# Position bias in eight transfers a layer, and VectorE's roots and rotary embeddings behind the attention weights

## The reference, cut to what matters

```python
def hybrid_layer(x, ...):                     # two of them
    h = rms_norm(x, norm_mix_g) * (1 + sc_m) + sh_m      # scale and shift come from c @ ada_w
    # one wide product h @ w_in gives q, k, v of three attentions, latents, and three gates
    o_na  = neighborhood_attention(...)       # 4 heads of 64, on a grid of 8 rows x 64 columns
    o_mla = blocked_attention(...)            # 4 heads, keys and values from a latent of 128
    o_gqa = blocked_attention(...)            # 8 query heads, 2 key heads, axial rotary embedding
    merged = sigmoid(ga)*(o_na @ w_br_na) + sigmoid(gb)*(o_mla @ w_br_mla) + sigmoid(gc)*(o_gqa @ w_br_gqa)
    x = x + g_m * (merged @ w_out)
    ...                                       # then a gated feed-forward block

def neighborhood_attention(q, k, v, rpb):     # rpb: (4 heads, 15 row offsets, 31 column offsets)
    s = einsum(q_row, k_band) * scale         # 16 queries of a row against 8 rows x 32 columns
    s = s + rpb[:, row_off][..., col_off]     # position bias
    s = where(col_valid, s, -inf)             # a window of 16 columns
    p = softmax(s)
```

## Time and profile before

| what | value |
|---|---|
| median of three runs | 2883.03 us |
| the profiled execution: its own time | 2883.88 us |
| the profiled execution: its span | 2882.1 us |
| granted TensorE clock, mean | 0.994 |
| VectorE busy | 1545.7 us (54%) |
| ScalarE busy | 677.5 us (24%) |
| GpSimd busy | 1659.0 us (58%) |
| DMA | 280.49 MB, mean 97 GB/s |
| `rpb_wide<-bias_copies` | 64 transfers of 24.0 KB |

### The profile page before, as it was taken

How to read it: one execution, slowest core, us unless ns; L and a number is a source line. 1 busy time by engine, 2 the same in 40 slices (tenths; PEclk the granted TensorE clock), 3 DMA queues, 4 the chain that set the end, 5 groups by cost and what they waited for, 6 DMA issues and landing times.

```text
span 2882.1 us, 44383 instructions
## 1 busy us (share of the span) xinstructions
PE 2825.3 (98%) x18030; PEld 2243.4 (78%) x18030; DVE 1545.7 (54%) x2283; ACT 677.5 (24%) x1158; POOL 1659.0 (58%) x1332
## 2 busy tenths in 40 slices
PE   8899999999999999999999999999999999999998
PEld 6666787888877767778888877877777787788886
DVE  6788876555225664444333275655566456662342
ACT  3444212000014443111000033233333433310000
POOL 4434577877765334586777744344344534676774
PEclk9999999999999999999999999999999999999999
DMA  7323543344332112232223221122112212222221
GB/s 278 106 94 125 195 163 125 138 153 148 129 103 80 37 59 67 72 118 85 98 95 102 98 82 49 59 67 69 56 62 69 70 47 69 81 95 95 99 98 59
DMA packets 97524, 280.49 MB, mean 97 GB/s; under 512 B 21278, under 2 KB 32286, under 8 KB 97182
## 3 DMA queue, kind: packets, MB, share of 16 engines
q1 hardware_dynamic: 85904, 274.70, 28.0%
q10 hardware_dynamic: 11438, 3.26, 0.6%
HBM read 275.76 MB, written 3.13 MB: 97 GB/s over the span
## 4 chain that ended last, share of the span: by engine, by line
PE 89%; DVE 7%; issue 1%; ACT 1%; ACTq 1%; DMA 0%; SPq 0%; DVEq 0%; POOL 0%; POOLq 0%
PE ps L358 25%; PE ps L360 24%; PE ps L359 24%; PE ps L1404 3%; PE ps L1212 2%; PE ps L1222 2%; PE ps L1242 2%; ACTq L618 1%; PE ps L1449 1%; DVE first_mod L1718 1%; PE ps L1037 1%; PE ps L1033 1%; PE ps L1034 1%; PE ps L1526 0%; DVE mg L1812 0%
## 5 line engine op out<-in xcount | busy, mean ns | idle before, releaser
L592 POOL TENSOR_TENSOR wR<-raw,wR 128x512 fp32r<-128x512 f32 (+1 forms) x866 | 1198.9, 1403 | 68.0 <-ACT wR L649 31.0
L588 POOL CAST wR<-raw 128x1024 fp32r<-128x1024 f32 (+3 forms) x462 | 465.8, 1008 | 1123.6 <-PE ps L360 1005.5
L358 PE MATMUL ps<-hR,wR 128*128 128x512 f32 x2224 | 903.8, 406 | 7.0 <-DVE hR L1739 6.8
L359 PE MATMUL ps<-hR,wR 128*128 128x512 f32 x2224 | 870.1, 391 | 0.0
L360 PE MATMUL ps<-hR,wR 128*128 128x512 f32 x2224 | 869.4, 391 | 0.0
L358 PEld LDWEIGHTS ps<-hR,wR 128*128 128x128 f32 x2224 | 419.2, 188 | 113.3 <-issue 21.6
L360 PEld LDWEIGHTS ps<-hR,wR 128*128 128x128 f32 x2224 | 419.1, 188 | 89.9
L359 PEld LDWEIGHTS ps<-hR,wR 128*128 128x128 f32 x2224 | 419.8, 189 | 82.2 <-issue 4.3
L1697 DVE SCALAR_TENSOR_TENSOR xT<-ps,lm,xT 128x512 f32<-128x512 f32 x32 | 24.0, 751 | 215.4 <-PE ps L360 215.4
L358 PE MATMUL ps<-act_f,wR 128*128 128x512 f32 x352 | 137.7, 391 | 0.0
L360 PE MATMUL ps<-act_f,wR 128*128 128x512 f32 x352 | 137.0, 389 | 0.0
(11 more groups left out here) (394 smaller groups left out, 4180.7 us busy)
## 6 DMA issues: line engine op xcount, KB each, us to landing
raw<-in_weights_dram SPq DMA_DIRECT2D x468, 512.0 KB, 3.3
first_mod<-in_weights_dram SPq DMA_DIRECT2D x16, 512.0 KB, 10.4
raw<-in_weights_dram SPq DMA_DIRECT2D x50, 128.0 KB, 2.4
raw<-in_weights_dram SPq DMA_DIRECT2D x16, 256.0 KB, 2.9
raw<-in_weights_dram SPq DMA_DIRECT2D x8, 384.0 KB, 10.4
xT<-in_x_dram SPq DMA_DIRECT2D x1, 2048.0 KB, 9.6
out_dram<-xT SPq DMA_DIRECT2D x4, 512.0 KB, 2.6
rpb_wide<-bias_copies ACTq DMA_DIRECT2D x64, 24.0 KB, 2.7
```

The lines of the kernel that those rows point to most:

```text
L358: mm(out, w_hi, r_hi, start=first, stop=False)
L359: mm(out, w_hi, r_lo, start=False, stop=False)
L588: nc.gpsimd.tensor_copy(wR[:, u, 0, 0:cols], raw[:, r % RING, 0:cols]).then_inc(hi_done, 1)
L592: ins = nc.gpsimd.tensor_tensor(wR[:, u, 1, part], raw[:, r % RING, part], wR[:, u, 0, part], ALU.subtract)
```

## The change

It does four things in each of the two hybrid layers.

1. The padded bias rows in DRAM are 64 elements wide (16 zeros, 31 values, 17 zeros), not 127. `rpb_wide` takes whole rows of 64, so that one piece of 8 rows x 64 elements (2 KB) is contiguous, and one transfer brings all four heads of a query row: 8 transfers of 128 KB a layer take the place of 32 of 24 KB. They are issued at the same places, 4 and 4.
2. Before step 0 VectorE masks only kinds 0 and 1 of pair 0. Kind 2 of pair 0 and all of pair 1 come in `between(1)`, ahead of `outputs(0)`.
3. `gk_root` (step 2), `rope(10)` (step 4) and `q_root(3, ...)` (step 6) move from `between` to `behind`, that is behind `weights_of`.
4. A late post whose next product is a short one (fewer than eight steps) goes ahead of `modulate`.

```diff
-BIAS_ROWS = 4 * 15 * 127
+BIAS_ROWS = 4 * 15 * 64
-NA_WIDE = 48
+NA_WIDE = 64
-    dram_bias = nc.dram_tensor("bias_rows", (DEPTH * 4 * 15, 127), F32, kind="Internal")
+    dram_bias = nc.dram_tensor("bias_rows", (DEPTH * 4 * 15, NA_WIDE), F32, kind="Internal")
-                rows = sb("rows", [DEPTH * 60, 127], into=r)
+                rows = sb("rows", [DEPTH * 60, NA_WIDE], into=r)
-            act.dma_start(rows[:, 48:79], rpb).then_inc(s_rows, 16)
+            act.dma_start(rows[:, NA_COLS:NA_COLS + 31], rpb).then_inc(s_rows, 16)
...
                 for row in range(first_row, end):
-                    for h in range(4):
-                        first = NA_COLS * BIAS_ROWS * l + (h * 15 + 7 - row) * 127 + GRID - 1 - NA_COLS
-                        act.dma_start(rpb_wide[16 * row:16 * row + 16, h],
-                                      bass.AP(dram_copies, first, [[BIAS_ROWS - 1, NA_COLS], [127, 8], [1, NA_WIDE]])).then_inc(s_bias, 16)
+                    first = NA_COLS * BIAS_ROWS * l + (7 - row) * NA_WIDE + NA_COLS - 1
+                    act.dma_start(rpb_wide[16 * row:16 * row + 16].rearrange("p h k e -> p h (k e)"),
+                                  bass.AP(dram_copies, first, [[BIAS_ROWS - 1, NA_COLS], [15 * NA_WIDE, 4], [1, 8 * NA_WIDE]])
+                                  ).then_inc(s_bias, 16)
...
-                def mask_bias(pair):
+                def mask_bias(pair, kinds):
-                    dve.wait_ge(s_bias, 512 * l + 512)
+                    dve.wait_ge(s_bias, 128 * l + 128)
-                    for kind, first in enumerate(BAND_TABLE):
+                    for kind in kinds:
+                        first = BAND_TABLE[kind]
...
-                mask_bias(0)
+                mask_bias(0, (0, 1))
...
                 def between(s):
-                    if s == 2:
-                        gk_root()
+                    if s == 1:
+                        mask_bias(0, (2,))
+                        mask_bias(1, (0, 1, 2))
                     elif s == 3:
                         ckv_root()
-                    elif s == 4:
-                        rope(10)
-                    elif s == 6:
-                        q_root(3, 0, 12, ((0, 8, 0.125), (8, 12, 96 ** -0.5)))
...
                 def behind(s):
                     if s == 2:
+                        gk_root()
                         rope(14)
                     elif s == 3:
                         latent(8, 7)
                     elif s == 4:
+                        rope(10)
                         latent(6, 2)
                     elif s == 5:
                         latent(7, 3)
                     elif s == 6:
+                        q_root(3, 0, 12, ((0, 8, 0.125), (8, 12, 96 ** -0.5)))
                         kr_rope()
...
-                    if s == 1:
-                        mask_bias(1)
                     behind(s)
+                    late = [p for p, early in ENDS[s] if not early and PRODS[p][0] in GATE_OF]
+                    soon = [p for p in late if PRODS[p + 1][2] < KD]
+                    for p in soon:
+                        post(p)
                     if l == 0:
                         rows_done = modulate(rows_done, DUE["step", s])
-                    for p, early in ENDS[s]:
-                        if not early and PRODS[p][0] in GATE_OF:
+                    for p in late:
+                        if p not in soon:
                             post(p)
```

## The result

| kernel | median us (lowest to highest, runs) | ratio to before, 95% interval |
|---|---|---|
| before | 2882.90 (2880.27 to 2886.25, 4) | |
| after | 2865.78 (2864.57 to 2867.14, 4) | 0.9942 (0.9930 to 0.9955) |

The change saves 17.1 us (0.58%), more than the 0.2% that can be told from nothing. The profiled execution of after took 2864.96 us, 18.9 less than that of before; its span is 2863.2 us.

The account below looks back on a forecast made before the run. TensorE, busy 98%, was taken as the bound, so time is won only from its stalls and low clock; 7.1 + 0.8 + 5.9 + 0.8 + 0.2 + 2.2 = 17.0 us off 2883.9 gives 2867, range 2861 to 2874.

Parts of the forecast that it names:

- part 1: Fewer bias transfers in layer 0: first weights transposed at 80.4 instead of 87.51, 7.1 us saved (ends 4.1 and 8.1).
- step 4: Layer 0, `rope(10)` moved behind the weights: TensorE's 3.13 us wait goes, 5.9 us saved (ends 2.9 and 5.9).
- part 4: Posts ahead of `modulate` at three places in layer 0: 0.75 us less waiting each, 2.2 us saved.
- Rival C: ScalarE's transfer issues cost by bytes, 2.4 us each, delaying the copies: about 2881 us, chance 0.05.
- Rival B: Low-clock stretch stays, from late step 4 weights or gaps before first scores: 3 us each, 2870 to 2873, chance 0.22.
- Landing: Layer 0's bias transfers: all there near 64 us, 3.4 us after the last issue at 60.5.
- rival D: Bias lands late, the eight transfers one behind the other: 2891 us at 5 us a transfer, chance 0.03.
- Masking: VectorE, before step 0: four of six additions take 3.4 us, done near 68, five us before the scores end.
- Part 2: Masking split, eight additions moved ahead of `outputs(0)`: nothing on the path.
- Step 2 of layer 0: `gk_root` moved behind the weights: TensorE's 0.36 us wait and longer transposes go, 0.8 us saved.
- Layer 1: Same stall of step 3 goes, 0.8 us saved; bias transfers ahead of its first scores give 0.2 us more.
- VectorE's slack at step 6: Layer 0: VectorE still arrives before TensorE at the maxima of step 6, by some 2 us.

Follow-up runs that it names:

- experiments 1 and 2: After with 32 transfers of 32 KB a layer, and with 16 of 64 KB, in place of 8 of 128 KB: 2874.28 and 2866.08 us.
- experiment 11a: Before, unchanged, profiled once more: 2883.98 us (one run).
- experiment 10: After with layer 0's `modulate` of step 3 moved behind the weights of step 4: 2865.05 us, ratio 0.9935.
- experiment 7: After with the masking as before: all six additions of pair 0 ahead of step 0, pair 1 behind `outputs(0)`: 2864.05 us, ratio 0.9940.
- experiment 11b: After, unchanged, profiled once more: 2869.37 us (one run).
- experiment 6: After with `gk_root` put back ahead of the weights of step 2: 2865.83 us, ratio 0.9942.
- experiment 5: After with `rope(10)` put back ahead of the weights of step 4: 2871.63 us, ratio 0.9961.
- experiment 8: After with the three late posts of layer 0 behind `modulate` again: 2868.03 us, ratio 0.9950.
- experiment 3: After with 32 transfers of 24 KB a layer in 192-byte pieces: 2875.06 us, ratio 0.9973.

## Why the prediction was right, and where its terms were off

Forecast 2867 us (2861 to 2874), 17.0 us below the profiled execution of before; measured 2865.78, 17.1 between the medians. The near equality is partly luck: the largest term, part 1, was too small by 1.8 us, those of step 4 and of part 4 too large by 1.0 and 0.3, and the profiles hold differences of the clock that belong to no term.

**The issue goes by the transfer.** The prediction chose 0.45 us between 0.31 and 2.4. Measured 0.44 and 0.53 at 128 KB; experiments 1 and 2 bear it out at 32 and 64 KB. Rival C is out. The price of the transfers, however, begins at a threshold: 16 would have done as well.

**Part 1: 7.1 forecast, 8.9 measured.** The failing sentence is "TensorE gains nothing before 69.86: it was running without a gap". The products now end at 68.31 (the last step of three passes begins at 67.47), 1.55 us earlier; the other 0.2 is in the way from there to the weights, 10.32 us instead of the 10.54 forecast. That TensorE ran without a gap was true of that one execution. It had 8 more slow passes than experiment 11a, whose profile shows the floor bare that the same issues lay under the products. Before's weights come at 87.5 with 14 or 6 slow passes, after's at 78.6 to 78.9 in all executions of after and its variants with 8 or 16 transfers, with 0 to 8 slow passes. They come no sooner with 0, since TensorE then stands 1.44 us at 60.08 for VectorE's next tile (experiment 10). But no profile of them has 14. In after these products set the pace (ScalarE waits 3.93 us for them before its copies), so by an estimate each pass beyond 8 would cost 0.20 us (0.43 us from pass to pass against 0.23), 1.2 us for 14, and the 8.9 would be 7.7. That the gain is far more than the clock's luck is shown; that all of the 1.55 us is the change's is not.

**The clock behind the gaps.** Rival B's second half, a low clock behind the 1.1 us of gaps, did not come: 1.00 from 68 to 80 us. The 1.24 us of layer 1 was the right guide. The count of slow passes after one and the same gap of 2.7 us was 14 and 6 in the two profiles of before and 8 in both of after. The Trainium skill (page "TensorE: Matmul & The Clock Gate", section "Part 1: The HAM clock gate") says that the number of slow matmuls of one kernel differs from run to run with where the chip's free-running judgement falls; the two profiles of before agree. A kernel should not be credited with such a difference.

**Landing.** Forecast near 64; VectorE's additions begin at 64.25, behind a wait of 1.13 us for the transfers. But experiment 7 had them at 66.43 and experiment 11b at 63.42: the landing moves by 3 us from run to run. In the first profile VectorE still stood 3.74 us before the maxima, so rival D is out.

**Masking.** 3.4 us forecast for four additions, 3.94 measured. GpSimd was at work for most of that time (63.18 to 65.98, and from 66.41 on). The Trainium skill (page "SBUF — State Buffer", section "🔬 SBUF: two separate sides") says that a VectorE operation with two inputs in SBUF and a GpSimd one that reads SBUF block each other fully for the length of an instruction. The traces agree as far as they go: in before six such additions took 3.22 us, 0.54 each, from 93.17 us on, where GpSimd worked for only 0.5 us, while after's 24 took 0.96 on the mean and up to 1.60 in layer 0. The rows of 64 elements cost nothing by themselves, since the shortest addition of layer 0 took 572 ns before and 574 after. Part 2 was costed at nothing and is worth nothing (experiment 7).

**Step 2 of layer 0: 0.8 forecast, 0.95 in its place, and nothing in the sum.** As experiment 6 shows, time won here is given back at step 4. The prediction added the two steps up as if they were independent.

**Step 4: 5.9 forecast, 4.89 measured.** The mechanism held, the gap and the clock behind it with it (experiment 5: 3.73 us and 0.50). VectorE's own part came as forecast: the weights of the two heads were out 3.0 and 4.1 us behind the start of the maxima (117.06 and 118.13, behind 114.02), where the prediction had 3.1 and 4.1 (125.2 and 126.2, behind 122.08). VectorE's timelines of before and of after, where the maxima of step 4 begin:

```profile
122.08 0.42 DVE L1922 CUSTOM_DVE_ANT_0 ps<-ps,bias 128x256 f32<-128x256 f32 x1
```

```profile
114.02 0.42 DVE L1923 CUSTOM_DVE_ANT_0 ps<-ps,bias 128x256 f32<-128x256 f32 x1
116.37 0.69 DVE L1943 TENSOR_TENSOR prob<-ps,rinv 128x512 f32<-128x512 f32 x1
117.44 0.69 DVE L1943 TENSOR_TENSOR prob<-ps,rinv 128x512 f32<-128x512 f32 x1
```

What failed is "TensorE, earlier by the 0.8 us of step 2". TensorE reached this step 9.83 us earlier than before (scores at 108.24 instead of 118.07) and VectorE only 8.06 (maxima at 114.02 instead of 122.08), so TensorE had gained 1.77 us on it and not 0.8. A wait of 0.95 us, named for ScalarE's copy, took the freed place. The prediction also left that copy of the turned values out, the operation queued behind the late exponentials. It did bound the rest rightly: "a stall that stays would be under one us". That is also just inside its own sign of being wrong, a new wait of over 1 us.

**Layer 1: 0.8 + 0.2 forecast.** Measured 0.93 for the step and 0.15 up to the first scores.

**Part 4: 2.2 forecast, 1.9 measured.** 0.75 a place was right (0.77 in experiment 8); that 0.3 would be given back at the scores of a later step was not foreseen.

**VectorE's slack at step 6.** Forecast "by some 2 us", measured 0.83 us of idle before those maxima. The direction was right, but less than half of the margin was there: VectorE is closer behind than the sums of its idle times told.

## What to carry to other kernels

Count the DMA issues in a compute engine's stream as instructions of about half a microsecond each, from 24 to 128 KB alike, and ask which copies stand behind them; merge them only until the engine waits for its input again. When a stall is removed, follow every engine's stream up to the freed place, since the wait named there afterwards may be a bystander (here ScalarE's copy, where taking 2.3 us of VectorE's work out from ahead of the maxima was what helped). Profile before twice: an engine that lags slightly behind a second floor hides it, and what looks like luck is then in part a gain of the change.

## What the runs showed that was not expected

- Sixteen issues a layer cost nothing that can be told over eight, and 32 cost 8.5 us: the price begins at a threshold between the two.
- Pieces of 192 bytes instead of 2 KB changed neither the time (0.8 us, within the spread) nor the landing (2.7 against 2.5 us) of transfers this small. The 128 KB transfers onto 16 partitions landed in 4.3 us, slower than 512 KB did in 3.4.
- After a gap of 2.7 us the same program ran 14 or 6 passes slowly, and experiment 3, with the same gap, none. In layer 0's first 130 us, gaps of 0.95 to 1.7 us never lowered the clock, and gaps of 3.1 to 7.9 us did each time; gaps of 2.2 to 2.7 us did in some executions and not in others.
- The clock between 1640 and 1760 us (1.00, or 0.92 to 0.99) separates two profiles of after by about 4 us, more than most parts of the change are worth.
